# Odd mixer: four constants loaded in the first expert block, keys turned beside the projection, queries summed before rotation, last squares one step later

## The reference

```python
def odd_mixer(x, w_in, gqa_q_norm, gqa_k_norm, cos_c, sin_c):
    q, k, v = _split(x @ w_in, ODD_SPLITS)
    q = rms_norm(q.reshape(b, s, GQA_HEADS, GQA_HEAD_DIM), gqa_q_norm)
    k = rms_norm(k.reshape(b, s, GQA_KV_HEADS, GQA_HEAD_DIM), gqa_k_norm)
    ...
    q = apply_rope(q, ...)
    k = apply_rope(k, ...)
    ...
    pr = jax.nn.softmax(sc.astype(jnp.float32), axis=-1)
```

## Time and profile before

| | us |
|---|---|
| median of 3 runs (2490.19 to 2491.40) | 2490.46 |
| profiled execution, its own time | 2495.82 |
| profiled execution, span | 2494.0 |
| TensorE busy (matmuls) | 2107.5 |
| VectorE busy | 1034.8 |
| ScalarE busy | 708.5 |

### The profile page before, as it was taken

The page is one execution under the profiler, slowest core; times in us unless marked ns, Lnnn a source line. Parts: engine busy times, 40 slices in busy tenths (PEclk is TensorE's granted clock), DMA queues, the critical chain, the costliest instruction groups (busy, mean ns, idle before and its releaser), DMA issues. The chain is left out here.

```text
span 2494.0 us, 31146 instructions
## 1 busy us (share of the span) xinstructions
PE 2107.5 (85%) x12583; PEld 1402.4 (56%) x12600; DVE 1034.8 (41%) x1526; ACT 708.5 (28%) x975; POOL 76.7 (3%) x146
## 2 busy tenths in 40 slices
PE   8779777777767887777767999988999999988998
PEld 6457322222235652222222888775888888766887
DVE  3346000000036630000001667665776776665776
ACT  3523100010015320000001433434333443434342
POOL 0000000000002000000000000010000000010000
PEclk9769998989889998989898999987999999988999
DMA  8103999999981369999999566431555456432551
GB/s 330 51 34 131 398 426 427 426 427 426 427 337 75 131 247 428 426 427 426 427 426 405 172 202 211 135 127 51 186 197 173 159 179 235 133 105 63 192 184 42
DMA packets 192681, 623.72 MB, mean 250 GB/s; under 512 B 17542, under 2 KB 114920, under 8 KB 159848
## 3 DMA queue, kind: packets, MB, share of 16 engines
q1 hardware_dynamic: 192616, 622.84, 64.6%
HBM read 621.76 MB, written 1.05 MB: 250 GB/s over the span
## 5 line engine op out<-in xcount | busy, mean ns | idle before, releaser
L1899 PE MATMUL psum<-weight_ring,arena 128*32 128x256 f32 x4096 | 290.1, 438 | 149.2 <-DMA weight_ring<-in_w 148.6
L2173 PE MATMUL psum<-x_both,up_hi 128*128 128x512 f32 x1408 | 359.6, 397 | 0.7 <-DVE x_both L456 0.6
L1899 PEld LDWEIGHTS psum<-weight_ring,arena 128*32 128x32 f32 x4096 | 135.2, 122 | 306.8 <-DMA weight_ring<-in_w 192.1
L1916 PE MATMUL psum<-weight_ring,arena 128*32 128x512 f32 x1024 | 247.8, 652 | 55.9 <-DMA weight_ring<-in_w 52.3
L2173 PEld LDWEIGHTS psum<-x_both,up_hi 128*128 128x128 f32 x1408 | 258.1, 188 | 58.9 <-DVE x_both L456 4.2
L1949 DVE TENSOR_TENSOR arena<-arena,psum 128x256 f32<-128x256 f32 x32 | 13.5, 422 | 545.9 <-PE psum L1899 545.9
L563 PE MATMUL psum<-w_hi,x_both 128*128 128x512 f32 (+2 forms) x800 | 213.0, 395 | 15.3 <-DVE mix_lo L695 10.1
L2221 DVE TENSOR_TENSOR up_lo<-weight_ring,up_hi 128x2048 fp32r<-128x2048 f32 x88 | 201.3, 2292 | 18.5 <-ACT up_hi L2195 18.2
L2176 PEld LDWEIGHTS psum<-x_both,up_lo 128*128 128x128 f32 x1408 | 192.3, 188 | 15.5
L2176 PE MATMUL psum<-x_both,up_lo 128*128 128x256 f32 x1408 | 197.1, 282 | 0.0
L2233 DVE TENSOR_REDUCE arena<-psum 128x256 f32<-128x512 f32 x176 | 113.4, 687 | 186.8 <-PE psum L2176 186.8
(11 more groups left out here) (318 smaller groups left out, 2439.9 us busy)
## 6 DMA issues: line engine op xcount, KB each, us to landing
weight_ring<-in_w SPq DMA_DIRECT2D x192, 2048.0 KB, 25.7
weight_ring<-in_ffn_wg SPq DMA_DIRECT2D x44, 1024.0 KB, 5.5
weight_ring<-in_ffn_wu SPq DMA_DIRECT2D x44, 1024.0 KB, 8.0
weight_ring<-in_ffn_wd SPq DMA_DIRECT2D x44, 1024.0 KB, 4.9
weight_ring<-in_w_in SPq DMA_DIRECT2D x12, 2048.0 KB, 8.1
weight_ring<-in_w_o SPq DMA_DIRECT2D x4, 2048.0 KB, 19.7
weight_ring<-in_ple_gate_w SPq DMA_DIRECT2D x4, 2048.0 KB, 11.9
weight_ring<-in_w_out SPq DMA_DIRECT2D x4, 2048.0 KB, 7.8
```

The source lines that it names most:

```text
L1899: last = pe.matmul(ps[j * CAP:(j + 1) * CAP, 4 + k // 2, 0:QW], tokens_now[:, cc, :], w[:, c, j * QW:(j + 1) * QW], start=cc == 0, stop=cc ...
L1916: last = pe.matmul(ps[j * CAP:(j + 1) * CAP, 6 + h, :], hc[:, i, j * CAP:(j + 1) * CAP], w[:, jj, i, h, :], start=i == 0, stop=i == 1)
L2173: last = pe.matmul(ps[:, 4 + 2 * f + h, :], w_part[:, f, h, c, :], x_both[:, :, c, :], start=c == 0, stop=False, skip_group_check=True)
```

## The change

Four small transfers (the two norm gains, the positions, the inverse frequencies) leave the odd mixer's `load` and are issued at the head of the first expert block's `load`, with a signal of their own, `odd_loaded`. They land in `chunk_masks` columns that the even mixer has done with, and in `positions`. VectorE's first parameter wait in the odd projection becomes a wait for that signal; a `params_ready` stands at k = 4 behind the keys. `gain_tables` moves from k = 0 to k = 2, the sum of the key squares from 4 to 3, the keys from 5 to 4, their transposes to TensorE at k = 4 and their copies to ScalarE at k = 5, and the sum of the first query squares ahead of their rotation. A one-element exponent behind the sines takes over the load of ScalarE's exponent table. The last squares go from step -1 of the attention to step 1 and their sum from step 1 to step 2.

```diff
+    odd_loaded = signal("odd_constants_loaded")
+    def load_odd_constants(sp):
+        for dst, src in ((gqa_gains[:, 0:HD], spread(t["gqa_q_norm"][0])), (gqa_gains[:, HD:2 * HD], spread(t["gqa_k_norm"][0])),
+                         (pos_i[:, :], t["positions_2"][0].rearrange("(a p) -> p a", p=P)),
+                         (inverse_frequencies, spread(t["c_inv_freq"]))):
+            sp.dma_start(dst, src, allow_slow_non_contiguous=True).then_inc(odd_loaded.sem, 16)
...
-            act.activation(rope_2[:, :, 0, :], self.absolute, ACT.Sin, scale=-1.0, bias=float(np.pi / 2))
+            act_chain.link(act, act.activation(rope_2[:, :, 0, :], self.absolute, ACT.Sin, scale=-1.0,
+                                               bias=float(np.pi / 2)))
+            act.activation(self.absolute[:, 0, 0:1], self.absolute[:, 0, 0:1], ACT.Exp)
...
-            load_params(sp, (gains[:, 0, :], spread(t["gqa_q_norm"][0])), (gains[:, 1, :], spread(t["gqa_k_norm"][0])),
-                        (ln_params[:, 0, :], spread(t["ln1_g"][1])), (ln_params[:, 1, :], spread(t["ln1_b"][1])),
+            load_params(sp, (ln_params[:, 0, :], spread(t["ln1_g"][1])), (ln_params[:, 1, :], spread(t["ln1_b"][1])),
                         (causal, t["c_causal"]), (group_mean, t["c_group_mean"]))
-            tables.load(sp)
...
+        def heads_on_tensor(pe, k):
+            if k == 4:
+                turn_keys(pe)
...
         def heads_on_scalar(act, k):
             if k == 2:
                 tables.sines(act)
             if k in (3, 5):
                 square_heads(act, k // 2 - 1)
+            if k == 5:
+                place_keys(act)
         def heads_on_vector(dve, k):
-            if k == 0:
-                gain_tables(dve)
             if k == 1:
                 tables.reduce_angles(dve)
+            if k == 2:
+                gain_tables(dve)
+            if k == 3:
+                sum_heads(dve, 0)
             if k == 4:
-                sum_heads(dve, 0)
+                finish_keys(dve)
+                params_ready(dve)
             if k == 5:
-                finish_keys(dve)
+                sum_heads(dve, 1)
                 rotate_heads(dve, 1).then_inc(rotated.sem, 1)
-                sum_heads(dve, 1)
...
                     place_queries(act, 0, 4, 3)
                     place_queries(act, 2, 5, 4)
+                elif step == 1:
                     square_last(act)
...
-                elif step == 1:
+                elif step == 2:
                     sum_heads(dve, 2)
...
             sp.wait_ge(mixed.sem, mixed.at(0))
+            if layer == 0:
+                load_odd_constants(sp)
             load_params(sp, (p_tokens, t["p"][layer, 0].rearrange("(a p) d -> p a d", p=P)),
```

More of the change, by code:

```diff
@@ L1389, in odd_mixer @@
         squares = mem.take(TILES * half_heads * HD)
-        gains = mem.take(2, HD)
         rope_gained = mem.take(2, 4, TILES * HD // 2)
@@ L1495, in place_queries, with turn_keys, place_keys @@
                      ).then_inc(placed.sem, 1)
+        def turn_keys(pe):
+            pe.wait_ge(doubled.sem, doubled.at(1))
+            for b in range(2):
+                for i in range(2):
+                    for a in range(TILES):
+                        last = pe.transpose(ps[:, 2 + b, i * SEQ + a * P:i * SEQ + (a + 1) * P],
+                                            k_twice[:, a, 2 * b + i].rearrange("p u d -> p (u d)"), ident[:, :])
+                last.then_inc(turned.sem, 1)
+        def place_keys(act):
+            for b in range(2):
+                act.wait_ge(turned.sem, turned.at(b + 1))
+                act.copy(k_cols[:, 2 * b:2 * b + 2, :], ps[:, 2 + b, :].rearrange("p (c q) -> p c q", c=2)
+                         ).then_inc(placed.sem, 1)
+        def heads_on_tensor(pe, k):
+            if k == 4:
+                turn_keys(pe)
         def heads_on_scalar(act, k):
```

35 lines of the change are left out of this document (13 added, 22 removed).

## The result

| | us |
|---|---|
| before, median of 3 runs, as in the prediction | 2490.46 |
| before, median of the 4 runs taken beside the change | 2490.74 |
| after, median of 4 runs (2469.61 to 2474.88) | 2470.86 |
| ratio, with its 95% interval | 0.9923 (0.9906 to 0.9940) |
| after, profiled execution and its span | 2469.79, 2468.0 |

A forecast was written before the change was run, and what follows sets the result against it. TensorE was taken to bound the odd projection, around a 10.39 us wait behind the late constants. The terms 13.07 - 1.03 + 1.00 + 0.9 = 13.94 took 2490.46 to 2476.5 us, range 2473.0 to 2480.5.

The forecast's parts named there:

- step 1: Odd mixer's projection: loading the four constants one expert loop earlier ends TensorE's wait and low clock, gaining 13.07 us.
- The transfers ahead of the tokens: First expert block: issuing the four transfers first costs SyncE 2 us but the kernel nothing; up to 2 us without cover.
- Rival (d): First expert block: parameters delayed by the four transfers ahead make the kernel slower, 2495 if landing at 228; chance 0.03.
- step 2: Odd projection: keys turned beside the last unit; transposes cost TensorE 1.03 us, given back as 1.00, scores 13.04 us earlier.
- steps 3 and 4: Odd attention: query sums ahead of rotation, table load moved, last squares after the second exponent; gain 0.6 to 1.2, taken 0.9.
- the meeting with POOL: Odd attention: two pairs of VectorE scalings fall into POOL's rotation, each stretched from 0.62 to 2.66 us.
- step 4: Odd attention: last squares after the second exponent; fourth pair of scores at 15.8 to 16.4 for 17.0, gain 0.9.
- What the mixer gains is therefore kept: Second expert loop: its six-slot ring refills as units are used, so the mixer's gain is kept through it.
- It starts earlier, as a whole: Second expert loop: claimed to start earlier as a whole, keeping the mixer's gain.
- The sum: Whole kernel: the terms add to a gain of 13.94 us, from 2490.46 to 2476.5.
- (a): Odd attention: POOL costs less or the clock stays 1.00 in the first scores; 1.6 to 4.5 us more, around 2473.5; chance 0.15.

The follow-up runs named there:

- squares_early: The changed kernel with the last squares back ahead of the attention and their sum back at its step 1; 2474.13 us, ratio 0.9935.
- layout_only: The kernel before with only the positions' allocation moved ahead of the arena, no instruction changed; 2483.76 us, ratio 0.9974.
- arena_back: The changed kernel with the positions allocated behind the arena again, the rest of the change kept; 2478.94 us, ratio 0.9956.
- before_again: The kernel before, unchanged, run for a second trace; 2489.64 us, ratio 0.9997.
- gap_64: The kernel before with 64 unused bytes ahead of the arena, so the same place within 64 bytes; 2491.83 us, ratio 1.0003.
- sum_step3_gap: The changed kernel with the last squares' sum at the attention's step 3 and the arena moved off the multiple of 64; 2475.49 us, ratio 0.9940.
- down_off_64: The changed kernel with the down weights' and hidden halves 32 bytes further, off the multiple of 64; 2469.85 us, ratio 0.9917.
- pad_66: The changed kernel with 66 more idle products on TensorE ahead of the second block; 2479.17 us, ratio 0.9954.
- sum_step3: The changed kernel with the sum of the last squares at the attention's step 3 instead of 2; 2469.97 us, ratio 0.9913.
- constants_only: The kernel before with the four small loads issued early under their own semaphore, also moving the positions' allocation; 2471.03 us, ratio 0.9917.
- warm_tail: The changed kernel with eight idle products on TensorE in its wait at the odd mixer's attention end; 2470.75 us, ratio 0.9921.
- warm_tail_sum: The changed kernel with eight idle products at the attention's end and the last squares' sum one step later; 2467.23 us, ratio 0.9903.
- all_three: The changed kernel with eight idle products, the later sum, and down weights' and hidden halves 32 bytes further; 2468.68 us, ratio 0.9912.

## Why the prediction was wrong

- **The stall** (step 1): right. Low part 2 no longer waits, the clock stays at 1.00, the halves start 5.6 us apart (727.95, 733.57, 739.19), and the sixth half starts at 751.46, 28.98 us behind the first products; without the keys ahead of it that is 27.95, forecast 752.77 - 724.95 = 27.82.
- **The transfers ahead of the tokens**: right. SyncE issued the four in 1.83 us, from 190.89 to 192.72, and nobody waited for them: TensorE takes the tokens at 207.56, two transposes behind the router and with no idle time of its own. Rival (d) did not happen.
- **The keys** (step 2): right. 1.03 on TensorE, scores 13.01 us nearer for 13.04.
- **Queries and last squares** (steps 3 and 4): the sum was right, 1.06 us for 0.9, and so was the meeting with POOL (2.59 and 2.64 for the forecast 2.66). The place was not: squares_early shows that step 4 gave none of it. The prediction put down under step 4 what was won without it, most of it by the steps ahead of it and the moved table load. Its 0.9 was followed with all of them in place, so that it came out says nothing for step 4 by itself.
- **"What the mixer gains is therefore kept"**: right for the expert loop behind it. From the third low part of the output weights to the second block's first products on up_hi it is 553.1 us before (829.04 to 1382.1) and 553.2 in the changed kernel (815.49 to 1368.7), and it changed by 0.7 us at most in all kernels but the padded one.
- **"It starts earlier, as a whole", and so the sum**: this is the step that failed. The sum took every stage that the diff doesn't name as unchanged, and so put at nothing what the moved allocation does. But the diff's first hunk moves an allocation, and with it the place of the weights' halves. The steps of the second block's loops took 8.32 us for 8.40. That is worth 6.7 us on the kernel before (layout_only) and 8.1 or 7.4 on the changed one (arena_back's 2478.94 less 2470.86 or 2471.57). With that put back, the time is 2478.9, and the forecast 2476.5 is 2.4 off, within its range.
- **Not foreseen in the mixer**: the fall of the clock at the attention's end, 3.3 us of the stage in both profiles of the changed kernel. With it the stage is 11.1 us shorter and not the 14.4 of arena_back. The second block's first mixer is 3.8 us shorter in the first of these profiles than before (32.15 for 35.94; the second traces have 32.18 and 35.12), which was not foreseen either and whose cause is open.
- **Which rival**: none. (a) had the nearest time, 2473.5, for a reason that did not occur: POOL cost what was forecast, and the clock fell to 0.50 between 764 and 765, so that the third pair of scores took 2.08 us, for the 1.13 of the fourth. The fourth pair of scores came at 15.94, in the forecast's 15.8 to 16.4.

SBUF — State Buffer in the Trainium skill ("Who interferes with whom") says that a `tensor_scalar` can take the shared port pair, and then it and GpSimd block each other for a whole instruction, and that a `tensor_reduce` never does. The traces agree: a pair of scalings took 2.59 and 2.64 us beside POOL's rotation and 0.62 behind it, and the sum beside it 1.22.

## What to carry to other kernels

An allocation that a change adds, drops or moves shifts every tensor behind it: compare the addresses of both programs, and take each long loop that reads the shifted tensors as changed until one run with the allocation alone moved says otherwise. When a gain is larger than its mechanism, look for it where the change does nothing: the period of a steady loop, read to a hundredth of a us in kernels with and without one part, found what no wait would have shown. With the moved allocation put back, as in arena_back, the forecast can be judged by itself. And a stage that is shorter in one trace is not yet a shorter kernel: the idle products won 3.3 us of the mixer in their trace, and the medians of four runs, with some 4 us to either side, can't tell whether the kernel gained it.

## What the runs showed of the hardware

The up products, matmuls of 128x128 float weights, took 2.5 ns longer (0.08 us over 32) when these weights' halves began 32 bytes beyond a multiple of 64 in a partition than when they began on one: a step of 8.40 us in before, before_again, arena_back, gap_64 and sum_step3_gap, and of 8.32 or 8.31 in the other kernels. In a kernel that issues 2816 of them that is 7 us of 2490. In the projections the same was worth 0.8 ns a product (0.02 us over 24). For the down products, whose weights are the hidden halves, the step shows no loss in down_off_64, though their six pairs take 2.79 us for 2.75.

TensorE waited 2.18 or 2.19 us at the attention's end (797.75 to 799.93 in the changed kernel). The granted clock fell to 0.50 (1.2 GHz) there in both profiles of the changed kernel (0.50 and 0.52 at 800 to 805), for a shorter time in pad_66 (0.74) and sum_step3 (0.69), and stayed at 1.00 in arena_back, down_off_64, squares_early and constants_only. Eight idle products in the wait kept it at 1.00 (2.4 GHz) in warm_tail, warm_tail_sum and all_three.
